# A two-layer hybrid encoder on one core: the last-but-one tile's output projection held back into the last tile's attention, its router input turned on TensorE, and its routing made in two parts

## What is computed

```python
h = rms_norm(x, norm_mix[l])
q_a, k_a, v_a, u_b, q_c, k_c, v_c, g_c = split(h @ w_in[l])          # 1024 -> 2048
y_a = sliding_window_sink_attention(q_a, k_a, v_a, q_norm, k_norm, sinks)   # 8 heads, window 128
y_b = multiscale_pool(u_b, pool_w, pool_scale)                       # windows 2, 4, 8, 16
y_c = retention(q_c, k_c, v_c, g_c, pos)                             # 4 heads, state carried from chunk to chunk
x = x + concatenate([y_a, y_b, y_c]) @ w_out[l]                      # 1024 -> 1024
x = x + moe_ffn(rms_norm(x, norm_ffn[l]), router_w, router_b, w_gate[l], w_up[l], w_down[l])
```

## Time and profile before

| | us |
|---|---|
| median of three runs | 3237.03 |
| profiled execution, its own time | 3266.3 |
| its span, first to last instruction | 3264.5 |
| TensorE busy | 3120.2 |
| DVE busy | 1468.6 |
| POOL busy | 1189.7 |
| ACT busy | 619.9 |

### The profile page before, as it was taken

One profiled execution on the slowest core, in us unless ns is written; L12 is line 12 of the kernel. 1 busy time (PEld: TensorE's weight loads), 2 busy tenths in 40 slices (PEclk: granted clock), 3 DMA queues, 4 the chain that ended last, 5 costly groups with the idle time before them and its releaser, 6 DMA issues.

```text
span 3264.5 us, 58551 instructions
## 1 busy us (share of the span) xinstructions
PE 3120.2 (96%) x20116; PEld 2428.5 (74%) x20116; DVE 1468.6 (45%) x4544; ACT 619.9 (19%) x1792; POOL 1189.7 (36%) x1308
## 2 busy tenths in 40 slices
PE   7999999999599999999989999999986999999998
PEld 4555565565499999999945565555554999999998
DVE  3566766766322222222236766767663222222221
ACT  4222222221111111111142221222221111111111
POOL 1322322213245555554322222213222455454444
PEclk9999999999799999999989999999997999999999
DMA  8222122121498999999942122121223899999996
GB/s 280 60 68 85 48 80 84 43 84 52 152 313 287 316 328 314 343 350 343 298 149 84 43 85 74 54 85 49 78 99 140 283 319 314 308 337 344 338 346 194
DMA packets 240678, 624.09 MB, mean 191 GB/s; under 512 B 63568, under 2 KB 133200, under 8 KB 207568
## 3 DMA queue, kind: packets, MB, share of 16 engines
q1 hardware_dynamic: 181584, 542.50, 46.7%
q0 software_dynamic: 58784, 77.70, 10.8%
HBM read 543.48 MB, written 77.73 MB: 190 GB/s over the span
## 4 chain that ended last, share of the span: by engine, by line
PE 88%; DVE 3%; DMA 3%; issue 2%; DVEq 1%; ACT 1%; SPq 1%; POOL 0%; ACTq 0%; POOLq 0%
PE bank L1437 30%; PE bank L1245 18%; PE bank L1465 15%; PE bank L1406 12%; PE bank L1236 3%; PE bank L1239 3%; PE bank L1209 2%; PE bank L1362 1%; PE bank L1383 1%; PE bank L1307 1%; DMA arena<-in_x 1%; DMA wts<-in_w_in 1%; DMA out<-arena 1%; ACT arena L741 1%; PE bank L1316 0%
## 5 line engine op out<-in xcount | busy, mean ns | idle before, releaser
L1437 PE MATMUL bank<-arena,wts 128*128 128x128 f32 (+7 forms) x8192 | 1004.0, 284 | 16.4 <-issue 10.1
L1437 PEld LDWEIGHTS bank<-arena,wts 128*128 128x128 f32 x8192 | 990.7, 191 | 24.3 <-issue 21.0
L1245 PE MATMUL bank<-wts,arena 128*128 128x512 f32 x1536 | 695.0, 599 | 40.8 <-DVEq L880 19.7
L1245 PEld LDWEIGHTS bank<-wts,arena 128*128 128x128 f32 x1536 | 281.5, 191 | 344.2 <-issue 322.8
L658 POOL DMA_INDIRECT out<-arena x296 | 463.3, 1565 | 171.5 <-issue 87.1
L1465 PE MATMUL bank<-arena,wts 128*128 128x128 f32 (+7 forms) x4096 | 499.4, 283 | 0.0
L1465 PEld LDWEIGHTS bank<-arena,wts 128*128 128x128 f32 x4096 | 493.4, 191 | 0.2 <-issue 0.2
L1406 PE MATMUL bank<-wts,arena 128*128 128x512 f32 x1024 | 453.4, 596 | 0.0
L1185 DVE TENSOR_TENSOR arena<-arena,bank 128x128 f32<-128x128 f32 (+6 forms) x64 | 19.1, 299 | 810.2 <-ACT arena L815 810.2
L1406 PEld LDWEIGHTS bank<-wts,arena 128*128 128x128 f32 x1024 | 192.8, 191 | 230.5 <-issue 215.0
L648 POOL DMA_INDIRECT arena<-hrows,arena x288 | 281.0, 976 | 173.0 <-issue 156.6
(11 more groups left out here) (198 smaller groups left out, 2881.7 us busy)
## 6 DMA issues: line engine op xcount, KB each, us to landing
wts<-in_w_gate SPq DMA_DIRECT2D x128, 1024.0 KB
wts<-in_w_up SPq DMA_DIRECT2D x128, 1024.0 KB
wts<-in_w_down SPq DMA_DIRECT2D x128, 1024.0 KB
arena<-out SPq DMA_DIRECT2D x184, 128.0 KB, 3.0
hrows<-arena SPq DMA_DIRECT2D x36, 512.0 KB, 3.8
out<-arena SPq DMA_DIRECT2D x36, 512.0 KB, 15.5
arena<-in_x SPq DMA_DIRECT2D x32, 512.0 KB, 6.9
wts<-in_w_in SPq DMA_DIRECT2D x8, 2048.0 KB, 14.2
```

Source lines behind the costliest of these rows:

```text
L1245: i = mm(bIP[n % 2][:, :], hT[:, d], win[:, n, d], start=(d == 0), stop=(d == DC - 1))
L1437: return mm(gu_at(f, k, w), lhs, xT[:, d, 0:w], start=start, stop=(d == DC - 1), skip_group_check=True)
```

## The change

- Step 15 no longer projects tile 14's output. TensorE does the first half of it at the start of step 16, ahead of turning tile 15's q and k, and the second half in two blocks of four products: one ahead of the scores, one behind the retention products. It needs tile 14's attention results only, which stand ready.
- Tile 15's own projection begins early: the first two products of each half (the pooling part) go behind the retention output. The others follow in the order: four of the first half, router parts of tile 14, the last two, the router's fold, six of the second half, rank.
- Tile 14's router input is turned on TensorE too, behind those first products. It isn't read back from memory, so SP issues 4 transfers fewer in a layer. DVE copies one half out of PSUM and then makes tile 14's norm, behind z and ahead of the copy of the retention result. ACT copies the other half. ACT's sum of squares of tile 14 moves from the end of step 15 to behind the copies of the turned probabilities.
- The DVE adds tile 14's first half behind the copy of the turned retention q and k, places tile 13 there (rank now in bank bA), and adds the second half behind the maxima.
- `route` is split into `pick_experts` and `weigh_experts`. For tile 14 the DVE picks, makes both adds of tile 15, and then weighs and places. ACT's router part of tile 14 goes behind its copy of the attention result.
- SP asks for the first expert's weights at the very start of step 16, ahead of the store of tile 14's x, and this store stands ahead of the store of its h.
- `project` gives both halves of every tile the same waits: output weights, pooling, attention, retention. Before, only the first half had them.

The core of the diff, TensorE:

```diff
+                    def project(t1, o, k, part):
+                        for n in range(*part):
+                            d = (4, 5, 0, 1, 2, 3, 6, 7)[n]
+                            if n == 0:
+                                e.wait_ge(wout_full, (l + 1) * 16)
+                                wait_alone(e, pool_ready, t1)
+                            if n == 2:
+                                e.wait_ge(attn_ready, t1)
+                            if n == 6:
+                                e.wait_ge(ycT_ready, t1)
+                            i = mm(bIP[k][:, :], dT[o][:, d - 4] if d in (4, 5) else mixT[:, d],
+                                   wout[:, d, 512 * k:512 * k + 512], start=(n == 0), stop=(n == DC - 1))
+                        if part[1] == DC:
+                            i.then_inc(pe_oproj, 1)
...
+                    if s == TILES:
+                        e.wait_ge(proj_ready, (t0 - 1) * 4 + 3)
+                        project(t0 - 1, b, 0, (0, DC))
                         e.wait_ge(kvd_read, t0 - 1)
+                        rank(t0 - 1, bA)
+                        e.wait_ge(proj_ready, (t0 - 1) * 4 + 4)
...
+                    if s == TILES:
+                        project(t0 - 1, b, 1, (0, 4))
...
+                    if s == TILES:
+                        project(t0 - 1, b, 1, (4, DC))
...
+                    if s == TILES:
+                        for k in range(2):
+                            e.wait_ge(x_new, (t0 - 2) * 2 + k + 1)
+                            project(t0, o, k, (0, 2))
+                        e.wait_ge(rank_read, t0 - 1)
+                        e.wait_ge(kvd_read, t0)
+                        h2T_turn(b)
...
-                    if back:
-
-                        e.wait_ge(wout_full, (l + 1) * 16)
-                        wait_alone(e, pool_ready, t0)
+                    if back and s < TILES - 1:
                         for k in range(2):
...
+                            e.wait_ge(proj_ready, t0 * 4 + 3 + k)
+                            project(t0, o, k, (0, DC))
                             if k == 0 and tail:
                                 rank(t0)
+                    elif s == TILES:
+                        project(t0, o, 0, (2, 6))
+                        router_parts()
+                        project(t0, o, 0, (6, DC))
+                        router_fold()
+                        project(t0, o, 1, (2, DC))
+                        rank(t0)
```

DVE (shortened in the same way) and ACT:

```diff
+                    if s == TILES:
+                        add_x(TILES - 1, b, 0)
+                        place(l, TILES - 1, o, bA)
                     if back:
                         e.wait_ge(pe_scores, t0)
...
+                    if s == TILES:
+                        add_x(TILES - 1, b, 1)
...
-                    if tail:
+                    if s == TILES:
+                        h2T_in()
+                        norm_2(TILES - 1, b)
+                    if tail and s != TILES:
                         route(l, s, b)
                     if back:
                         e.wait_ge(pe_ycT, t0)
                         v.tensor_copy(mixT[:, 6:8].rearrange("p j n -> p (j n)"), bE[:, 0:256]).then_inc(ycT_ready, 1)
+                    if s == TILES:
+                        pick_experts(l, s)
...
+                    elif s == TILES:
+                        add_x(s, o, 0)
+                        add_x(s, o, 1)
+                        weigh_experts()
                         place(l, s, b)
...
+                        if s == TILES:
+                            sumsq_new(TILES - 1, b)
+                            h2T_in()
```

More of the change, by code:

```diff
@@ L448, in step @@
                         rest()
[L449 to L457 removed]
+                    if back and s != TILES - 1:
+                        store_x(s, b)
                 def load_weights(i, b, n=None):
@@ L751, in step, with router @@
                             folded(1)
-                    if tail:
-                        if not (front or back):
-                            e.wait_ge(pe_h2T, l + 1)
-                            a(h2T[:, 4:8], bB[:, :].rearrange("p (d n) -> p d n", d=4), ACT.Copy).then_inc(h2T_half, 1)
+                    def router():
                         e.wait_ge(pe_parts, t0 - 1)
@@ L760, in step, with sumsq_new, h2T_in @@
                         a(es, bA[:, 256:288], ACT.Exp, scale=stat[:, 1:2]).then_inc(exp_router, 1)
+                    def sumsq_new(s, o):
+                        e.wait_ge(x_new, (l * TILES + s) * 2)
+                        a(squares, xr[o], ACT.Square, accum_out=stat[:, 4:5]).then_inc(sumsq_2, 1)
+                    def h2T_in():
+                        e.wait_ge(pe_h2T, l * 2 + s - TILES + 1)
+                        a(h2T[:, 4:8], bB[:, :].rearrange("p (d n) -> p d n", d=4), ACT.Copy).then_inc(h2T_half, 1)
+                    if tail and not back:
+                        h2T_in()
+                    if tail and s != TILES:
+                        router()
                     if back:
@@ L1251, in y_at, with rank @@
                         return (bE, bF)[a][:, 256 + 64 * j:320 + 64 * j]
[L1253 removed]
+                    def rank(t0, bank=bE):
                         e.wait_ge(picks_ready, t0 - 1)
[L1256 to L1261 removed]
+                        mm(bank[:, 384:416], before, pick, start=True, stop=True)
+                        mm(bank[:, 416:448], ones, pick, start=True, stop=True).then_inc(pe_rank, 1)
@@ L1321, in step @@
                         i.then_inc(pe_scores, 1)
-                    if tail and not (front or back):
+                    if s == TILES:
+                        project(t0 - 1, b, 1, (4, DC))
+                    if tail and not back:
                         e.wait_ge(x_new, (t0 - 1) * 2)
-                        for d in range(DC):
-                            dst = (bA, bB)[d // 4][:, (d % 4) * P:(d % 4) * P + P]
-                            for a in range(4):
-                                at = a * PIECE + d * 32
-                                i = mm(dst[32 * a:32 * a + 32], xr[b][:, at:at + 32], ident, start=True, stop=True)
-                        i.then_inc(pe_h2T, 1)
+                        e.wait_ge(kvd_read, t0 - 1)
+                        h2T_turn(b)
                     chunk(1)
@@ L1332, in step @@
                         fold(1)
-                    if tail:
-                        e.wait_ge(h2T_ready, t0 - 1)
-                        if not (front or back):
-                            e.wait_ge(h2T_half, l + 1)
-                        for d in range(DC):
-                            i = mm(bA[32 * (d % 4):32 * (d % 4) + 32, 0:P], rw[:, d], h2T[:, d], start=(d < 4), stop=(d >= 4))
-                        i.then_inc(pe_parts, 1)
+                    if tail and s != TILES:
+                        router_parts()
                     chunk(2, (0, 4))
-                    if tail:
+                    if tail and front:
                         e.wait_ge(parts_read, t0 - 1)
```

146 lines of the change are left out of this document (81 added, 65 removed).

## The result

The changed kernel took 3217.6 us (median of six runs, 3213.2 to 3220.3), the kernel before 3237.8 us beside it: a ratio of 0.9939, with a 95% interval of 0.9929 to 0.9949. It is 20 us faster, where 21.9 were forecast (3215.5 us).

What follows compares the result with a forecast made beforehand. TensorE, busy 96%, bounds the kernel, with pauses at each mixing phase's end. Gains of 10.6 us (layer 0) and 11.3 (layer 1), together 21.9, take 3237.0 to 3215.1, rounded up to 3215.5; range 3211 to 3227.

Steps and rivals of the forecast that it cites:

- hand-overs: Some 15 changes between engines in the walk, at 0.05 to 0.1 us each; 1.0 us taken off the gain in layer 0.
- Steps 1 and 2: Tile 14's projection around tile 15's turnings and scores: turnings start at 800.2, projection ends at 810.3, DVE's add and placing hidden.
- Step 3: DVE sets the pace from second add through z, ending 819.9; TensorE's work beside it ends near 818.5, cover 1.5 us.
- Step 4: Products with v and attention copy, ending 822.0; ACT's squares and turned-x copy ahead of that copy cost a 0.5 us detour.
- Steps 5 and 6: TensorE's remaining projection ends 833.1; beside it DVE's routing and adds, placing ending 836.9, DVE late by 0.7 us.
- The yardstick of before: Old kernel's stretch from tile 14's projection to DVE's copy of tile 15's turned x: 56.3 us, 57.0 in layer 1.
- Edits costed at nothing: SP's earlier weight request, the store order, and new waits in the second half of middle tiles' projection: nought.
- rival D: New waits in the projection's second half in 28 middle tiles make it slower; 3246 at 1.1 us each; chance 0.05.
- The turning on TensorE: Tile 14's x turned on TensorE instead of loads and DVE turning: 64 small products, 1.96 us added, run under cover.
- Rival A: Clock drops at the thin place (818.5 to 822.0) in both layers, costing 2.5 to 5 us each; 3223; chance 0.17.
- Rival B: DVE becomes the bound in the last tile's stretch, about 2 us a layer lost; 3219.5; chance 0.12.
- Rival C: Clock stays low from 806 through tile 15's projection, giving back 9 to 12 us a layer; 3237, no change; chance 0.06.

Runs made afterwards that it cites:

- e7: Changed kernel with ACT copying the attention result ahead of tile 14's sum of squares and turned x, and the DVE making tile 14's norm later; 3215.1 us.
- e5: Changed kernel with SP asking for the first expert's weights behind the stores of tile 14's x and h, as before; 3277.3 us (kernel before on that chip 3299.6).
- e3: Changed kernel with tile 14's router input read back from memory and turned on the DVE, without its turning on TensorE; 3222.7 us.
- e10: Kernel of e3, but TensorE turns tile 14's x nevertheless and nobody reads the result; 3271.6 us, on a chip where the kernel before took 3299.6.
- e1: Changed kernel with the second half of tile 14's projection in one block ahead of the turnings of tile 15's q and k; 3224.0 us, ratio 0.9961.
- e11: Kernel before with 42 useless products of 128 columns in TensorE's pauses in step 16; 3290.4 us beside 3299.6, ratio 0.9977.
- e8: Kernel of e7, but for tile 15 ACT copies both halves of the turned x and the DVE goes to the norm at once; 3217.1 us.
- e4: Changed kernel with the first two products of each half of tile 15's projection made with the others, not early; 3221.7 us, ratio 0.9956.
- e9: Kernel of e8 with tile 14's router products and fold earlier, and its experts weighed ahead of the adds; 3211.3 us, ratio 0.9921.
- e2: Changed kernel with tile 14's routing in one part, weights made ahead of tile 15's two adds; 3279.2 us, on a chip where the kernel before took 3299.6.
- e0: Kernel before, unchanged, run once more for a second profile; 3235.2 us.

## Why the prediction was right

It stands on one walk through the new order, so it can be held against the trace, counted from the start of tile 14's projection (792.17 in the prediction, which is the list's 792.01 and 0.16; in the changed kernel the list has 792.68, so I count from 792.84):

| event | foretold | measured |
|---|---|---|
| turnings of q and k begin | +8.0 | +8.3 |
| tile 14's projection over | +18.1 | +18.6 |
| z ready | +27.7 | +27.9 |
| attention result copied | +29.8 | +30.3 |
| TensorE's projections over | +40.9 | +41.7 |
| both adds of tile 15 over | +42.1 | +43.5 |
| copy of tile 15's turned x | +44.7, with hand-overs +45.7 | +46.0 |

- **Steps 1 and 2** hold: two blocks of 3.6 us among the scores, and the DVE's add and placing (803.1 to 805.6) under the first of them.
- **Step 3** has the right time and a margin that isn't there. The DVE sets the pace from 811.5 to 816.6. Then TensorE's turning of tile 14's x, which the walk lets run free under cover, has to wait for the DVE's state (0.38 us), and the chain goes on through it:

```profile
815.14 1.23 DVE arena L991
...
816.75 1.95 PE bank L1317 x64
818.70 1.04 PE bank L1261 x8
819.76 0.60 ACT arena L794
```

  TensorE waits 1.2 us ahead of the products with v, but for ACT's copies, which end at 820.85, level with z at 820.75. The 1.5 us of cover in the prediction leave these copies out: with them its own numbers (819.5 and 819.9) leave 0.4.
- **Step 4**, the detour on ACT: 0.5 us, confirmed by e7. In the trace it is this order (squares, half of the turned x, attention result):

```profile
821.01 1.06 ACT L769 ACTIVATE arena<-arena 128x1024 bf16<-128x1024 f32 x1 [0.17 <-issue]
...
822.07 0.58 ACT L774 ACTIVATE arena<-bank 128x512 f32<-128x512 f32 x1
822.55 0.59 ACT L804 ACTIVATE arena<-bank 128x512 f32<-128x512 f32 x1
```

- **Steps 5 and 6** hold in their order. From the attention result's copy to the end of the projections it took 0.3 us more than foretold, from there to the end of the adds 0.6 more. Each hand-over was priced at nothing in the walk. All the differences sum to 1.3 us at the copy, for which 1.0 had been taken off. The DVE is late by 0.5 us at the end (0.7 foretold).
- **The yardstick of before.** The term least well sized was not of the new kernel but of the old: 56.3 us in its first profile, 57.6 in its second, since the clock rises at another point. By two profiles the gain of the stretch is 10.2 to 11.5 us in layer 0 and 10.9 to 11.2 in layer 1. That is 21.2 to 22.7, against 21.9 foretold and 20 (3237.8 less 3217.6) and 22 (3237.9 less 3216.1) measured. That 21.9 lies in the middle of this is in part luck: the prediction took its yardstick from one profile and didn't know that it varies.
- **Edits costed at nothing.** SP's order is nothing within about 1 us, by e5. Of rival D a middle tile of the changed kernel shows the two halves:

```profile
642.17 7.03 PE L1331 MATMUL bank<-wts,arena 128*128 128x512 f32 x16
...
649.40 7.11 PE L1331 MATMUL bank<-wts,arena 128*128 128x512 f32 x16
```

  They begin 7.23 us apart, and 7.23 in the same tile before; the second half with its new waits is as dense as the first. Over the 14 tiles of layer 0 TensorE's idle time ahead of these instructions is 93.5 us without a visible cause in both kernels, 5.3 for ACT in both, and 0.7 for the DVE against 0.6. D is excluded, by the trace; no kernel was run for it.
- **The turning on TensorE** was counted as a cost under cover, with the loads and the turning that it replaces as removed. e3 and e10 show the reverse: the way is worth nothing, and the work itself 1.0 to 2.1 us a layer. The sum was right because the walk went at the full clock throughout, and this turning is part of what kept it there. The reason given for the clock, density, is borne out by e1, e3, e10 and e11; by e8 it is no certainty.
- **Rival A** didn't happen in the changed kernel (two profiles, four layers), but its place and its mechanism are right. With that place thinned (e3, e4) or left nearly as it was (e8, one layer of two) the clock fell and cost 1.0 to 2.1 us, below the 2.5 to 5 of the rival; only e1, which is thin ahead of it as well, reached them in one layer (3.3). The rival has the slow turning on the chain, as e1 and e4 show it, but lets 1.5 us of it hide, and nothing of it hid. Its sum is too high all the same, because in no run were the turnings, the products with v and the projection's first block slow together. The block alone, which the rival has at 0.3 us by the earlier trace rows, cost 1.5 to 2.0 where it was slow (e1, e3, e8). The Trainium skill, page "TensorE: Matmul & The Clock Gate", section "A second HAM failure mode: psum-queue depth-cycling", says that TensorE's frequent short idles between groups of matmuls made its clock swing in another kernel. This was set against the change, and in the changed kernel's two profiles the clock stays at 1.00 over five such idles of 0.4 to 1.3 us; in one layer of e8 it did fall.
- **Rival B** is in part what happened. Its signs are there: TensorE waits 0.38 us for the DVE at 816.4, the adds begin at 835.1, and from 829.94 on the chain of the profile is the DVE's. Its price of 2 us a layer is not: the copy came 0.3 us behind the forecast (46.0 for 45.7). The two medians, 3217.6 and 3216.1, lie between the forecast's 3215.5 and B's 3219.5, so the times alone don't tell them apart. **Rival C** is refuted: the clock is at 1.00 throughout.

## What to carry to other kernels

When the last iteration of a pipelined loop has lost the work that used to fill it, look for work one iteration back whose inputs are ready and whose result is wanted late; walk the new order with the durations of a dense iteration, not of the loose one, and take off about 0.1 us for each change of engine (1.3 us over some 13 to 15 here). Fillers pay twice, by covering waits and by keeping TensorE at its full clock, so price a "free" removal of work by what runs slow behind the pause that it leaves. Then look which engine has no gap left: here it was the DVE, and taking a copy from it and making its weights earlier, with ACT's order turned (e7 to e9 together), was worth 5 us more.

## What the runs showed of the hardware that I had not expected

- The clock fell behind a pause of 3.16 us (e3) and also with pauses of 1.2 us only (e8, one layer), while the changed kernel kept it over pauses as long in four layers. A fall of the clock cost what ran slow on the chain: 1.5 us behind the longest pause (3.87 us, e4), and 1.7 us behind a short one (e8), so the length of the pause did not set the price.
- Some waits for TensorE's signal were longer on one chip. The runs e2, e5, e10 and e11 shared a chip on which the kernel before took 3299.6 us, against 3236 and 3238 on the two others. On it ACT began its copies at the start of the expert phase 5.8 us behind the last modelled product, which is 0.06 us elsewhere. ACT in e2, with TensorE's group before it:

```profile
874.83 1.14 ACT L820 ACTIVATE arena<-bank,par 128x128 f32<-128x128 f32 x4 [15.18 <-remote]
```

```profile
865.68 3.35 PE L1521 MATMUL bank<-cst,arena 128*32 128x128 f32 x64 [10.21 <-DMA arena<-hrows,row]
```

  The first profile of the kernel before shows a like delay of 4.0 to 4.5 us (a gap of 22.7 to 23.2 us from the last cast to the expert phase, 18.6 to 18.7 in e0), and slower expert phases with it. In both layers of e2 and e10 and in layer 1 of e5 the DVE began its mask 1.4 us later than elsewhere behind the retention products (3.59 us of wait for 2.22). Which mechanism it is stays open. It seems to add about the same to kernels before and after: e5, one run of nearly the changed kernel, took 22 us less than the kernel before on this chip, as the changed kernel does on the others (20 and 22). The changed kernel itself was not run there.
